# Relative bias added by VectorE, turned queries and probabilities, and prompt logits from raw rows

## The chip, the cores and the metric

The kernel runs on one core of one Trainium2 chip. The metric is the device time of one execution in microseconds (us). TensorE, VectorE, ScalarE and GpSimd compute, SyncE's queue issues the loads of the weights, and 16 DMA engines move them.

## The reference

One step of a two-layer trunk over 128 context tokens (the prompt, t = 0 in the kernel) and 128 latent tokens (the sample, t = 1), width 1024, all in float32. Layer 0 has grouped-query and differential attention, layer 1 neighbourhood attention of 16 heads: the sample's queries see 128 cached context keys and 128 latent keys inside a window, and the latent scores get a learned relative bias per head. Each layer ends in a mixture of 16 experts, two of them per token.

```python
s_lat = jnp.einsum('brqhd,brkhd->brhqk', qg, kw) * scale + bias   # then -inf outside the window
s_ctx = jnp.einsum('brqhd,bkhd->brhqk', qg, ctx_k) * scale
p = jax.nn.softmax(jnp.concatenate([s_ctx, s_lat], axis=-1), axis=-1)

h = rmsnorm(x, g) * (1.0 + scale_c) + shift_c      # per channel, from the condition
scores = jax.nn.softmax(h @ w_router, axis=-1)     # then the choice of group and of two experts
hid = silu(h @ w_gate[e]) * (h @ w_up[e]); y += gate * (hid @ w_down[e])
```

## The kernel before

Every engine has its own program, and semaphores join them. The weights, 486 MB in all, stream through a ring of six slots of 2 MB and a few borrowed buffers. SyncE's queue loads a slot as soon as the unit that held it has been read: `load` for dense units, `load_early` and `load_in_turn` for the experts' (L475), which wait for TensorE's count of finished units, `moe_used`. Experts come in eight pairs a layer: gather of the tokens (L932), gate and up products (L971), transposes, down products, scatter (L941).

Attention goes by eight turns a layer, four of the sample and then four of the prompt, four heads each. In turn j TensorE transposes the probabilities of j (`probs_transposed`, through `transposes`, L699), computes the scores of j + 2 (`scores`, L812 and L817), and multiplies the values of j (`values`, L855 or L863). VectorE takes the maxima (L1484), ScalarE the exponentials (L1211), VectorE the division by the sums (L1504), ScalarE the copies out of PSUM (L1222). Between these TensorE does the jobs that the table `FILL` writes down by hand: input projections, products of the modulation (`mod`, L721), output projections (`wo`, L770). The relative bias comes from memory with the queries of each grid row in reversed order. In layer 1's sample turns a product with the permutation `rev8` (which also holds 1/SCALE) turns each head's bias and adds it onto the scores in PSUM (L817).

Behind the last turn is the tail. For the sample: normed rows transposed (`hT`), modulated on the way out of PSUM, logits (`rt`, L875), transposes back into token rows (`hk`, L699). For the prompt, once the output projection has completed x: sum of squares on ScalarE (L1133), power on GpSimd, normed rows on VectorE (L1395), transposes on TensorE, modulation half on ScalarE (L1144) and half on VectorE (L1402), logits, maximum (L1411, L1412), exponential (L1152), and VectorE's choice of experts (L1594 to L1605). Then `positions` counts places in the expert lists (L888 to L892); in layer 1 it first issues 12 products that nobody reads (`keep_busy`, L743), and `experts` issues 8 more of them in front of the first gather. In layer 0 the products of the next layer's modulation stand among the tail's jobs, and its transposes (`nextT`, L732) ahead of `positions`. PSUM has one bank for sums, and seven are handed out in the order of the jobs; `EMPTIED_BY` names the engine that frees each.

## Time and profile before

| | us |
|---|---|
| median of 3 runs | 1283.19 |
| lowest and highest | 1282.77, 1284.61 |
| the profiled execution, its time | 1283.81 |
| its span on the core | 1282.0 |
| PE busy | 1183.7 (92%) |
| DVE busy | 279.4 (22%) |
| ACT busy | 188.4 (15%) |
| DMA, mean over the span | 383 GB/s |
| chain that ended last | PE 72%, DMA 18%, issue 5%, DVE 2% |

PE is TensorE, PEld its weight loads, DVE VectorE, ACT ScalarE, POOL GpSimd, SPq SyncE's queue. L with a number is a line of the kernel. A busy TensorE also holds the time in which a product is slower than it could be. The DMA share is the mean over the 16 engines; it reads 1.0 or a little over where they are full. PEclk is the granted clock of TensorE, 1.00 at 2.4 GHz and 0.50 at 1.2. A product of float32 operands is kept as two records, a transpose as one. Times of the trace are counted from the start of the span.

### The profile page before, as it was taken

How to read it: one execution, taken by the hardware profiler on the slowest of the kernel's cores; microseconds unless marked ns; L12 is line 12 of the kernel's file. 1: busy time of each engine (PE TensorE's matmuls, PEld its weight loads, DVE VectorE, ACT ScalarE, POOL GpSimd, SP SyncE). 2: the span in 40 equal slices, each digit the busy share in tenths (PEclk: the TensorE clock that was granted, in tenths of full speed). 3: DMA queues.
4: the chain of work that ended last, by engine and by line, in shares of the span. 5: the costliest groups of instructions: out<-in, count | busy, mean ns of one | idle time of the engine just before them, and what ended most of it. 6: DMA issues, size and time to landing. Idle time of an engine off the chain costs nothing.

```text
span 1282.0 us, 13868 instructions
## 1 busy us (share of the span) xinstructions
PE 1183.7 (92%) x5519; PEld 517.6 (40%) x5519; DVE 279.4 (22%) x672; ACT 188.4 (15%) x437; POOL 49.4 (4%) x57
## 2 busy tenths in 40 slices
PE   4999989999889898989899999999998899889898
PEld 2545454343333334333344554743433334343333
DVE  1156441201021010101413433412020110101013
ACT  1234221000000100000121342210000001000010
POOL 0502000000000000000011100000000000000000
PEclk9999999999999999999989999899999999999999
DMA  9959999999999999999991579889999999999995
GB/s 376 333 201 386 423 408 424 429 392 427 430 428 427 430 427 430 428 427 429 408 330 57 207 279 415 324 353 424 374 429 427 429 427 429 429 427 430 427 428 230
DMA packets 57647, 491.62 MB, mean 383 GB/s; under 512 B 5090, under 2 KB 6258, under 8 KB 26884
## 3 DMA queue, kind: packets, MB, share of 16 engines
q1 hardware_dynamic: 55408, 485.92, 91.4%
q0 software_dynamic: 2016, 4.94, 1.3%
q8 instruction: 29, 0.48, 0.1%
q10 hardware_dynamic: 180, 0.17, 0.0%
q14 instruction: 14, 0.11, 0.0%
HBM read 488.26 MB, written 2.75 MB: 383 GB/s over the span
## 4 chain that ended last, share of the span: by engine, by line
PE 72%; DMA 18%; issue 5%; DVE 2%; ACT 1%; SPq 1%; POOL 1%; DVEq 0%; ACTq 0%; POOLq 0%
PE bank L971 42%; DMA ring<-in_w_gate 11%; PE bank L752 11%; DMA ring<-in_w_up 5%; PE bank L770 3%; PE bank L941 3%; PE bank L932 3%; DMA ring<-in_w_in_ab 2%; PE bank L721 2%; PE bank L699 2%; PE bank L992 1%; PE bank L1021 1%; PE bank L812 1%; PE bank L1005 1%; PE bank L875 1%
## 5 line engine op out<-in xcount | busy, mean ns | idle before, releaser
L971 PE MATMUL bank<-ring,hT 128*64 128x512 f32 x2816 | 638.6, 608 | 63.7 <-issue 30.0
L971 PEld LDWEIGHTS bank<-ring,hT 128*64 128x64 f32 x2816 | 213.3, 140 | 464.5 <-issue 462.7
L752 PE MATMUL bank<-ring,hT 128*128 128x512 f32 (+1 forms) x352 | 149.5, 583 | 4.7 <-DMA ring<-in_w_in_ab 2.4
L752 PEld LDWEIGHTS bank<-ring,hT 128*128 128x128 f32 x352 | 67.1, 193 | 80.0 <-issue 76.6
L1694 DVE TENSOR_TENSOR work<-work,bank 128x512 f32<-128x512 f32 x56 | 38.5, 687 | 193.6 <-PE bank L941 193.4
L1687 DVE TENSOR_TENSOR work<-work,bank 128x512 f32<-128x512 f32 x32 | 22.0, 687 | 236.5 <-PE bank L971 236.5
L1728 DVE COPY work<-bank 128x512 f32<-128x512 f32 x16 | 11.1, 692 | 225.6 <-PE bank L971 209.3
L932 PE MATMUL bank<-work 128*128 128x128 f32 x512 | 59.8, 275 | 0.0
L932 PEld LDWEIGHTS bank<-work 128*128 128x128 f32 x512 | 58.6, 192 | 0.0
L770 PE MATMUL bank<-ring,work 128*128 128x512 f32 x128 | 56.3, 594 | 0.0
L1274 ACT ACTIVATE hT<-bank 128x512 f32<-128x512 f32 x32 | 19.0, 595 | 248.3 <-PE bank L1021 248.3
L941 PE MATMUL bank<-work 128*128 128x512 f32 x112 | 51.8, 605 | 0.0
L721 PE MATMUL bank<-ring,cond 128*32 128x512 f32 x384 | 47.0, 623 | 1.6 <-DMA ring<-in_w_mod 1.2
L1300 ACT ACTIVATE work<-bank 128x512 f32<-128x512 f32 x16 | 9.6, 597 | 220.3 <-PE bank L971 193.0
L1675 DVE TENSOR_TENSOR work<-work,bank 128x512 f32<-128x512 f32 x32 | 22.0, 688 | 83.4 <-ACT work L1283 83.4
L971 PE MATMUL bank<-work,hT 128*64 128x512 f32 x152 | 39.2, 593 | 0.0
L770 PEld LDWEIGHTS bank<-ring,work 128*128 128x128 f32 x128 | 23.8, 190 | 28.7 <-issue 28.6
L1287 ACT ACTIVATE work<-bank 128x256 f32<-128x256 f32 x16 | 6.2, 385 | 196.4 <-PE bank L1040 196.4
L1283 ACT ACTIVATE work<-bank 128x512 f32<-128x512 f32 x32 | 19.1, 597 | 94.5 <-PE bank L971 94.5
L941 PEld LDWEIGHTS bank<-work 128*128 128x128 f32 x112 | 20.1, 189 | 31.5 <-issue 31.5
L1211 ACT ACTIVATE work<-bank,nm 128x256 f32<-128x256 f32 (+1 forms) x64 | 26.1, 421 | 29.9 <-DVE nm L1486 29.9
L1420 DVE TENSOR_REDUCE hss<-bank 128x8 f32<-128x512 f32 (+1 forms) x16 | 10.5, 657 | 88.8 <-ACT bank L1170 88.8
(195 smaller groups left out, 688.5 us busy)
## 6 DMA issues: line engine op xcount, KB each, us to landing
ring<-in_w_gate SPq DMA_DIRECT2D x64, 2048.0 KB, 17.0
ring<-in_w_up SPq DMA_DIRECT2D x56, 2048.0 KB, 17.2
ring<-in_w_down SPq DMA_DIRECT2D x56, 2048.0 KB, 16.9
ring<-in_w_mod SPq DMA_DIRECT2D x23, 2048.0 KB, 11.9
work<-in_w_up SPq DMA_DIRECT2D x8, 2048.0 KB, 17.8
ring<-in_w_in_c SPq DMA_DIRECT2D x6, 2048.0 KB, 20.2
ring<-in_w_in_ab SPq DMA_DIRECT2D x4, 2048.0 KB, 21.5
ring<-in_w_down SPq DMA_DIRECT2D x8, 1024.0 KB, 16.3
```

Source lines behind the costliest of these rows:

```text
L699: ins = pe.transpose(b[:, i * P:(i + 1) * P], src, K("ident"))
L721: ins = pe.matmul(out, cond[:, 2 * k + r, :], cols, start=(k, r) == (0, 0), stop=(k, r) == (3, 1), tile_position=(0, 32 * j))
L752: ins = pe.matmul(b[:, 0:n], hT[:, c, t * P:(t + 1) * P], w[:, c, 0:n], start=c == 0, stop=c == DC - 1)
L770: ins = pe.matmul(b[:, :], oT(l, t, c), w[:, c, :], start=c == 0, stop=c == DC - 1)
L932: ins = pe.matmul(bank[h][:, c * P:(c + 1) * P], htok(t)[:, at:at + P], pick[:, t, :], start=t == 0, stop=t == 1)
L941: pe.matmul(bank[4 + 2 * t + h][:, :], GT[:, t, :], yd[:, h * UC:(h + 1) * UC], start=True, stop=True).then_inc(m["scattered"], 1)
L971: ins = pe.matmul(bank[banks[j]][64 * e:64 * e + 64, :], lhs[:, 4 * h + c, 64 * e:64 * e + 64], weights(e, c, j), start=(h, c) == (0, 0), ...
L1211: ins = act.activation(PR[:, j % 2, h, 0:nk], bank_of(("S", l, t, b, e))[:, i * nk:(i + 1) * nk], ACT.Exp, bias=nm[:, j % 2, h:h + 1], sca ...
L1283: act.activation(sg[:, h * UC:(h + 1) * UC], bank[h][:, :], ACT.Sigmoid).then_inc(m["sig_done"], 1)
L1675: dve.tensor_tensor(hid[:, half], sg[:, half], bank[h][:, :], ALU.mult).then_inc(m["gate_taken"], 1)
L1687: dve.tensor_tensor(hid[:, half], hid[:, half], bank[2 + h][:, :], ALU.mult).then_inc(m["hid_done"], 1)
L1694: dve.tensor_tensor(y[:, t, cols], y[:, t, cols], bank[4 + 2 * t + h][:, :], ALU.add).then_inc(m["y_added"], 1)
```

## The change

The bias is masked and scaled once on VectorE with keys as they lie and queries still reversed, so the queries are reversed instead: in layer 1's sample the transposes of the queries (two banks, eight chunks) become products with the permutation `rev`, and so rows of scores come out reversed. VectorE adds the bias to the scores in PSUM before it takes the maxima, and the products with the bias go. The transposes of these turns' probabilities become products with `rev` too, which puts the order right.

In both layers the prompt's logits no longer wait for its normed and modulated rows. Raw rows of x are transposed (`xT`) and copied by ScalarE and VectorE, a bank each; the router's weights are scaled once by the modulation's scale (`wr0`), and the products of its shift with the router's weights (`rc`) are added after the logits have been multiplied by the rows' inverse norm. The modulation of the prompt's rows (`hT`, all eight parts now on ScalarE) and its token rows (`hk`) come behind the logits. In layer 1 the sample's logits move ahead of the second half of the prompt's output projection. In layer 0 `nextT` moves behind `positions`, and VectorE's part of it behind the count of rounds. `keep_busy` is as it was.

The core of the diff, without the context lines and the new declarations:

```diff
-    block("rev8")[:] = (row == back[None, :]) / SCALE
+    block("rev")[:] = row == back[None, :]
...
-    block("negrev")[:] = np.where(inside, 0.0, MASKED * SCALE)[back, :]
+    block("negrev")[:] = np.where(inside, 0.0, MASKED)[back, :]
...
-        7: [("hT", 1, 1), ("wo", 0, 0), ("rt", 1), ("wo", 1, 0), ("mod", 1, 0, 1),
-            ("hT", 1, 0), ("mod", 1, 0, 2), ("rt", 0), ("mod", 1, 0, 3), ("nextT",), ("pos",)]},
+        7: [("hT", 1, 1), ("wo", 0, 0), ("rt", 1), ("wo", 1, 0), ("rc",), ("mod", 1, 0, 1), ("xT",), ("mod", 1, 0, 2),
+            ("rt", 0), ("hT", 1, 0), ("mod", 1, 0, 3), ("hk", 0), ("pos",), ("nextT",)]},
...
-        7: [("hT", 1, 1), ("wo", 0, 0), ("wo", 1, 0), ("rt", 1), ("hT", 1, 0), ("rt", 0), ("pos",)]}}
+        7: [("hT", 1, 1), ("wo", 0, 0), ("rt", 1), ("wo", 1, 0), ("rc",), ("xT",),
+            ("rt", 0), ("hT", 1, 0), ("hk", 0), ("pos",)]}}
...
     def engine(name):
...
-            return ("act", "dve")[name[4]]
+            return "act" if name[2:4] == (1, 0) else ("act", "dve")[name[4]]
+        if kind == "xT":
+            return ("act", "dve")[name[2]]
+        if kind == "rt":
+            return ("dve", "act")[name[2]]
...
+            def turned(name, parts):
...
+                b = bank_free(name)
+                for i, src in enumerate(parts):
+                    ins = pe.matmul(b[:, i * P:(i + 1) * P], src, K("rev"), start=True, stop=True)
+                ins.then_inc(filled, 1)
...
+                if (l, t) == (1, 1):
+                    pe.wait_ge(ld_const, 16)
...
-                    transposes(("T", l, t, i), p)
+                    (turned if (l, t) == (1, 1) and i < 2 else transposes)(("T", l, t, i), p)
...
-                biased = (l, t) == (1, 1)
-                if biased and j == 0:
-                    pe.wait_ge(ld_const, 16)
-                    pe.wait_ge(bias_masked, 1)
...
-                                        start=True, stop=not biased, tile_position=(64 * e, 0))
-                        if i == 1 and not biased:
-                            ins.then_inc(filled, 1)
-                    for e in range(2) if biased else ():
-                        ins = pe.matmul(banks[e][:, i * nk + P:(i + 1) * nk], K("rev8"), bias[:, 4 * b + 2 * i + e, :],
-                                        start=False, stop=True)
+                                        start=True, stop=True, tile_position=(64 * e, 0))
...
-                    transposes(("PT", l, t, b, k), [PR[:, j % 2, h, kc * P:(kc + 1) * P] for kc, h in chunks[k * per:(k + 1) * per]])
+                    (turned if (l, t) == (1, 1) else transposes)(
+                        ("PT", l, t, b, k), [PR[:, j % 2, h, kc * P:(kc + 1) * P] for kc, h in chunks[k * per:(k + 1) * per]])
...
             def logits(l, t):
...
+                if t == 0:
+                    pe.wait_ge(router_scaled, l + 1)
...
-                    pe.wait_ge(*emptied_by(("hT", l, 1, t, h)))
+                    pe.wait_ge(*emptied_by(("hT", l, 1, 1, h) if t else ("xT", l, h)))
...
-                    ins = pe.matmul(b[:, 0:NE], hT[:, c, t * P:(t + 1) * P], wr[:, c, :], start=c == 0, stop=c == DC - 1)
+                    ins = pe.matmul(b[:, 0:NE], hT[:, c, t * P:(t + 1) * P], (wr if t else wr0)[:, c, :], start=c == 0, stop=c == DC - 1)
...
+                if t == 1:
+                    token_rows(l, 1)
...
+            def token_rows(l, t):
...
+                    pe.wait_ge(*emptied_by(("hT", l, 1, t, h)))
...
+            def shift_logits(l):
...
+                pe.wait_ge(mod_ready, 2 * l + 2)
+                pe.wait_ge(ld_router, 32)
+                b = bank_free(("rc", l))
+                for c in range(DC):
+                    ins = pe.matmul(b[:, 0:NE], modc[:, l, 2, 0, c:c + 1].to_broadcast([P, P]), wr[:, c, :], start=c == 0, stop=c == DC - 1)
+                ins.then_inc(filled, 1)
...
+            def rows_transposed(l):
+                pe.wait_ge(x_ready, 8 * l + 4)
+                for h in range(2):
+                    transposes(("xT", l, h), [channels(x[:, 0, :], 4 * h + i) for i in range(4)])
...
-                last = number["pos", l]
+                last = number["modT", 1, 0] if l == 0 else number["pos", 1]
...
-                for c in range(4):
-                    ins = act.activation(hT[:, c, t * P:(t + 1) * P], bank_of(name)[:, c * P:(c + 1) * P], ACT.Identity,
+                for c in range(8 if (kind, t) == (1, 0) else 4):
+                    if c == 4:
+                        ins.then_inc(emptied["act"], 1)
+                        name = ("hT", l, 1, 0, 1)
+                        act.wait_ge(filled, fill(name))
+                    ins = act.activation(hT[:, c, t * P:(t + 1) * P], bank_of(name)[:, c % 4 * P:(c % 4 + 1) * P], ACT.Identity,
...
+            def rows_transposed(l):
+                name = ("xT", l, 0)
+                act.wait_ge(filled, fill(name))
+                act.activation(hT[:, 0:4, 0:P], bank_of(name)[:, :].rearrange("p (c q) -> p c q", c=4), ACT.Copy).then_inc(emptied["act"], 1)
...
             def router(l, t):
...
-                name = ("rt", l, t)
...
-                act.activation(sco[:, t, :], bank_of(name)[:, 0:NE], ACT.Exp, bias=st2[:, t:t + 1],
-                               accum_out=st2[:, 2 + t:3 + t]).then_inc(emptied["act"], 1)
-
+                ins = act.activation(sco[:, t, :], bank_of(("rt", l, 1))[:, 0:NE] if t else lg[:, :], ACT.Exp, bias=st2[:, t:t + 1],
+                                     accum_out=st2[:, 2 + t:3 + t])
+                ins.then_inc(emptied["act"] if t else prompt_scored, 1)
...
+            def token_rows(l, t):
...
-                if l == 0:
-                    router(0, 1)
+                router(l, 1)
+                token_rows(l, 1)
...
-                if l == 1:
-                    router(1, 1)
+                rows_transposed(l)
+                router(l, 0)
...
-                router(l, 0)
...
+                token_rows(l, 0)
...
+                if group == 2:
+                    dve.wait_ge(mod_ready, 2 * l + 2)
+                    dve.wait_ge(ld_router, 32)
+                    dve.tensor_tensor(wr0, wr[:, :, :], modc[:, l, 3, 0, :].unsqueeze(2).to_broadcast([P, DC, NE]), ALU.mult).then_inc(router_scaled, 1)
...
+            def prompt_rows(l):
...
+                name = ("rc", l)
+                dve.wait_ge(filled, fill(name))
+                dve.tensor_copy(rc[:, :], bank_of(name)[:, 0:NE]).then_inc(emptied["dve"], 1)
+                name = ("xT", l, 1)
+                dve.wait_ge(filled, fill(name))
+                dve.tensor_copy(hT[:, 4:8, 0:P], bank_of(name)[:, :].rearrange("p (c q) -> p c q", c=4)).then_inc(emptied["dve"], 1)
...
             def largest_logit(l, t):
...
-                then(dve.tensor_reduce(st2[:, t:t + 1], bank_of(name)[:, 0:NE], AX.X, ALU.max))
+                if t == 0:
+                    dve.wait_ge(*emptied_by(("rc", l)))
+                    dve.scalar_tensor_tensor(out=lg[:, :], in0=bank_of(name)[:, 0:NE], scalar=ss[:, 0:1], in1=rc[:, :],
+                                             op0=ALU.mult, op1=ALU.add).then_inc(emptied["dve"], 1)
+                    dve.wait_ge(*emptied_by(name))
+                then(dve.tensor_reduce(st2[:, t:t + 1], bank_of(name)[:, 0:NE] if t else lg[:, :], AX.X, ALU.max))
...
-                dve.tensor_tensor(bias, bias, K("negrev").unsqueeze(1).to_broadcast([P, 16, P]), ALU.add).then_inc(bias_masked, 1)
+                dve.scalar_tensor_tensor(out=bias, in0=bias, scalar=1.0 / SCALE, in1=K("negrev").unsqueeze(1).to_broadcast([P, 16, P]),
+                                         op0=ALU.mult, op1=ALU.add).then_inc(bias_masked, 1)
...
+                if (l, t) == (1, 1):
+                    if j == 0:
+                        dve.wait_ge(bias_masked, 1)
+                    for e in range(2):
+                        name = ("S", l, t, b, e)
+                        dve.wait_ge(filled, fill(name))
+                        s = bank_of(name)[:, 0:2 * nk].rearrange("p (h k) -> p h k", h=2)[:, :, P:2 * P]
+                        ins = dve.tensor_tensor(s, s, bias[:, 4 * b + e:4 * b + e + 3:2, :], ALU.add)
+                    then(ins)
...
             def router(l):
...
-                for t in range(TT):
-                    dve.wait_ge(*emptied_by(("rt", l, t)))
+                dve.wait_ge(*emptied_by(("rt", l, 1)))
+                dve.wait_ge(prompt_scored, l + 1)
...
-                if l == 0:
-                    mod(1, 0)
...
+                if l == 0:
+                    mod(1, 0)
...
-                if l == 0:
-                    largest_logit(0, 1)
+                largest_logit(l, 1)
...
-                if l == 1:
-                    largest_logit(1, 1)
+                prompt_rows(l)
...
-                modulate(l, 1, 0)
...

```

## Rows read from the trace of the kernel before

**Rows 1.** Windows, layer 1: busy us (instructions) per engine, PEclk, DMA share, GB/s

```profile
675.00:700.00 25.00, 25.00 (x78) 12.52 (x77) 9.02 (x8) 4.95 (x10) 5.46 (x1) 1.00 0.00 1
...
828.00:837.00 9.00, 9.00 (x52) 4.17 (x50) 0.00 (x0) 1.19 (x2) 0.00 (x0) 1.00 0.17 66
...
900.00:930.00 30.00, 30.00 (x160) 12.99 (x158) 2.06 (x3) 2.88 (x5) 0.00 (x0) 1.00 0.91 370
```

**Rows 2.** Windows of layer 0's first pairs, same columns

```profile
200.00:260.00 60.00, 60.00 (x290) 23.22 (x288) 10.88 (x20) 5.65 (x10) 0.00 (x0) 1.00 1.01 429
...
260.00:290.00 30.00, 30.00 (x160) 12.86 (x158) 2.06 (x3) 2.88 (x5) 0.00 (x0) 1.00 0.95 387
```

**Rows 3.** Timeline of SyncE's queue: start us, us, instruction

```profile
814.44 0.39 SPq L523 DMA_DIRECT2D m<-in_w_down  x1
...
837.19 0.80 SPq L475 DMA_DIRECT2D ring<-in_w_down  x2
```

**Rows 4.** Timeline, TensorE in attention: start, us, instruction, idle before it

```profile
85.72 2.00 PE L812 MATMUL bank<-work 64*128 64x256 f32 x16
...
724.74 1.04 PE L699 MATMUL bank<-const,work 128*128 128x128 f32 x8
...
725.71 0.70 PE L812 MATMUL bank<-work 64*128 64x256 f32 x4
...
728.25 1.09 PE L863 MATMUL bank<-work 128*64 128x128 f32 x16
...
749.46 1.04 PE L699 MATMUL bank<-const,work 128*128 128x128 f32 x8
```

**Rows 5.** Timeline of VectorE in layer 1's attention, same columns

```profile
728.28 1.27 DVE L1484 TENSOR_REDUCE nm<-bank 128x2 f32<-128x512 f32 x2
...
741.12 0.42 DVE L1513 COPY work<-bank 128x256 f32<-128x256 f32 x1
```

**Rows 6.** Timeline of layer 1's tail, all engines, same columns

```profile
808.17 1.85 PE L875 MATMUL bank<-wr,hT 128*128 128x16 f32 x16
...
809.16 0.69 DVE L1538 TENSOR_TENSOR x<-x,tmp 128x512 f32<-128x512 f32 x1
...
809.87 1.07 PE L699 MATMUL bank<-const,hT 128*128 128x128 f32 x8
...
812.35 1.15 PE L699 MATMUL bank<-const,tmp 128*128 128x128 f32 x8 [1.42 <-DVE tmp L1395]
...
813.16 1.51 ACT L1144 ACTIVATE hT<-bank,modc 128x128 f32<-128x128 f32 x4 [1.32 <-PE bank L699]
...
815.08 3.57 PE L875 MATMUL bank<-wr,hT 128*128 128x16 f32 x16 [1.58 <-ACT hT L1144]
...
818.89 0.15 DVE L1412 TENSOR_SCALAR st<-st 128x1 f32<-128x1 f32 x1
...
820.22 3.29 PE L743 MATMUL bank<-const 128*128 128x128 f32 x24
...
823.41 0.40 PE L888 MATMUL bank<-chosen,const 128*128 128x16 f32 x2
...
826.41 3.74 PE L932 MATMUL bank<-work 128*128 128x128 f32 x32
```

**Rows 7.** Windows around the clock's fall and rise, columns of rows 1

```profile
814.00:815.00 1.00, 0.00 (x0) 0.00 (x0) 0.98 (x4) 0.67 (x2) 0.00 (x0) 0.67 0.73 307
...
821.00:822.00 1.00, 1.00 (x10) 1.00 (x9) 0.90 (x5) 0.07 (x1) 0.00 (x0) 0.92 1.06 442
```

**Rows 8.** Timeline of layer 0's tail, TensorE

```profile
169.80 1.92 PE L721 MATMUL bank<-ring,cond 128*32 128x512 f32 x16
...
173.89 1.15 PE L699 MATMUL bank<-const,tmp 128*128 128x128 f32 x8 [2.17 <-DVE tmp L1395]
...
183.59 0.37 PE L888 MATMUL bank<-chosen,const 128*128 128x16 f32 x2 [0.57 <-issue]
...
186.57 3.74 PE L932 MATMUL bank<-work 128*128 128x128 f32 x32
```

More of the change, by code:

```diff
@@ L43 @@
 for _name, _n in (("ident", P), ("mhalf", HD),
-                  ("upper", P), ("ones", P), ("iota", CAP), ("selg", 8), ("rev8", P),
+                  ("upper", P), ("ones", P), ("iota", CAP), ("selg", 8), ("rev", P),
                   ("negrev", P), ("low4", 16), ("cos", HD), ("ssin", HD), ("thr", ROUNDS_MAX - 1),
@@ L150, in banks_of @@
         return [("hT", l) + rest + (h,) for h in range(2)]
+    if kind == "xT":
+        return [("xT", l, h) for h in range(2)]
+    if kind == "hk":
+        return [("hk", l, rest[0], h) for h in range(2)]
     if kind == "rt":
-        return [("rt", l, rest[0])] + [("hk", l, rest[0], h) for h in range(2)]
+        return [("rt", l, rest[0])] + (banks_of(l, ("hk", 1)) if rest[0] else [])
     return [(kind, l) + rest]
@@ L164 @@
 EMPTIED_BY = {"vecT": "dve", "bT": "dve", "modT": "dve", "T": "act", "S": "act", "PT": "act",
-              "O": "dve", "oT": "act", "gb": "act", "wo": "dve", "hk": "act", "rt": "act", "pos": "dve"}
+              "O": "dve", "oT": "act", "gb": "act", "wo": "dve", "hk": "act", "rc": "dve", "pos": "dve"}
 def pt_jobs(l, t, b):
@@ L206, in engine @@
         if kind == "hT":
-            return ("act", "dve")[name[4]]
+            return "act" if name[2:4] == (1, 0) else ("act", "dve")[name[4]]
+        if kind == "xT":
+            return ("act", "dve")[name[2]]
+        if kind == "rt":
+            return ("dve", "act")[name[2]]
         if kind == "qkv":
@@ L247, in build @@
         br = sb("br", [P, NE])
+        rc = sb("rc", [P, NE])
+        lg = sb("lg", [P, NE])
         ss = sb("ss", [P, 4])
@@ L264, in build @@
         cnt8 = sb("cnt8", [P, TT * NG])
+        wr0 = cmq[:, :].rearrange("p (c e) -> p c e", c=DC)
         rounds = sb("rounds", [P, 1], I32)
@@ L353, in build @@
         max_ready, shared, o_ready = (sem(n) for n in ("max_ready", "probs_shared", "o_ready"))
+        prompt_scored = sem("prompt_scored")
+        router_scaled = sem("router_scaled")
         logit_max, mask_ready, rounds_ready = (sem(n) for n in ("logit_max", "mask_ready", "rounds_ready"))
@@ L894, in meanwhile @@
             def meanwhile(l, point):
-                job = {"in": project, "modT": mod_transposed, "gb": gate_rows, "wo": out_project, "rt": logits,
+                job = {"in": project, "modT": mod_transposed, "gb": gate_rows, "wo": out_project, "rt": logits, "hk": token_rows,
                        "oT": outputs_transposed, "hT": norm, "T": heads_transposed, "pos": positions}
@@ L901, in meanwhile @@
                         mod_transposed(1, 0)
+                    elif item[0] in ("rc", "xT"):
+                        {"rc": shift_logits, "xT": rows_transposed}[item[0]](l)
                     else:
```

## Prediction

> **What bounds the kernel now.** I read four views in this order. The windows by stage show first where the DMA engines stand still. In layer 1 they are idle for the whole of 675 to 700 and for most of 828 to 837, and 9% short between 900 and 930, while TensorE's share is full in all three [rows 1]. In layer 0 they are at 1.01 up to 260 and only from 260 to 290 a little short, 0.95 of 30 us, some 1.5 us [rows 2]. Where the DMA is full the weights set the pace, and an earlier TensorE is worth nothing there; time comes off only where the DMA waits for TensorE. The queue of SyncE, second, says what ends the large hole: after the load of 814.44 the next one goes out at 837.19, when the first product of pair 0 has given its slot back [rows 3]. So a shift of layer 1's first product by X moves that load, and with it all that follows, by X, in either direction; a gain is passed on up to about 8 us. In layer 0 a later first product is passed on too, since the DMA is already caught at 260 to 290, an earlier one by 1.5 us at most. Third, TensorE's rows of layer 1's attention have no gap but the few tenths of us before L863, so there its own work counts [rows 4, 5]. Fourth, the tail from the output projection to the gather: waits on VectorE and ScalarE, and a stretch at half clock [rows 6, 7].
>
> **Layer 1's attention.** Removed: 16 products with the bias. A turn of scores with them runs from 725.71 to the values' products at 728.25, 2.5 us [rows 4]; layer 0's two turns without them take 2.00, 1.0 a turn [rows 4]. Four turns: 4 x 1.5 = 6.0 us less. Added: 40 chunks (8 of queries, 32 of probabilities) are turned by a full product in place of a transpose. Eight transposes take 725.71 - 724.74 = 0.97 us, 0.12 each [rows 4]. The nearest product of that shape is the gather, 32 records for 16 products in 3.74 us, 0.23 each [rows 6]; the trace keeps two records for a float32 product and one for a transpose. So 40 x 0.11 = 4.4 us more. The lower end is nothing (if a turn costs what a transpose does), the upper the pace of the bias products, 0.3 each, +7.5 us; I take the gather's row, since it too runs one 128x128 product after another. Net -1.6 us.
>
> The Trainium skill, "TensorE: Matmul & The Clock Gate" (Terms), says that transpose mode is four times faster for float32. By that rule a turned chunk costs four transposes, 0.48 us, and the edit adds 40 x 0.36 = 14.4 us. The gather's row stands against it with not quite twice, and the row decides; the rule stays as a rival.
>
> VectorE gets two additions a turn over 128x256 of a score bank, 0.42 each by the copy of that size out of PSUM [rows 5], and a wait behind them: some 0.95 us a turn between scores and maxima. Queued behind it are the maxima (0.64 us each), the exponentials and, a turn later, the transposes. I cost it at nothing: scores of turn 2 are read at 728.28 and their transposes start only at 749.46, behind two projections of 7 us [rows 4, 5]; turns 0 and 1 have such projections in front too, turn 3 (scores at 737, transposes 754) one of them. Without that cover it would be 4 x 0.95 = 3.8 us. The mask becomes one operation in place of one: nothing. The scaled router weights wr0 (one more operation on VectorE in layer 1's scale group) stand just ahead of the last copy that the output projection waits for: about 0.35 us later, from 0.2 to 0.4. In layer 0 it is under cover. Attention: -1.6 + 0.35 = -1.25 us.
>
> **Layer 1's tail, in the times of before.** The logits of the sample and their token rows, 809.87 - 808.17 = 1.70 and 0.97 us, move ahead of the second half of the output projection; x is complete 2.67 us later, at 809.85 + 2.67 = 812.5 [rows 6]. The shift's logits (16 records, 1.70) fill TensorE up to then: nothing. Eight transposes of x to 813.5; ScalarE and VectorE copy a bank each (0.7), VectorE to 814.45; logits of the prompt on TensorE 814.45 to 816.15, at full clock. Before, they began at 815.08 and took 3.57 at half clock [rows 6]. Maximum, exponential, selection: before, the sign change is at 818.89, 0.4 after the logits, and the first product of the positions at 823.41, 4.52 later [rows 6]. After, with one operation more, the sign change is at 816.8 and the choice is ready at 821.3, 2.1 us earlier. But positions now stands behind something else. VectorE's copy and three small operations put the normed rows at 816.2, their transposes end at 817.15, the exponential leaves ScalarE at 817.3, and ScalarE alone now does the eight modulations, 3.0 us where it did four in 1.51 beside VectorE's four [rows 6]: to 820.35. The second four transposes of token rows end at 820.95. Then come the 12 idle products ahead of the positions (L743, 24 records), which the diff leaves, 12 x 0.23 = 2.8 us: to 823.75. Positions start at 823.75 against 823.41, and from there to the gather it is 3.0 us as before. Tail: +0.35 us. The gain of the raw rows is lost behind the modulations and the idle products.
>
> **Layer 0.** The output projection ends at 169.80 [rows 8]; shift logits to 171.5, modulation products (1.9) to 173.4, transposes of x to 174.35, modulation products to 176.25, logits to 177.95, sign change 178.6, choice 183.15. Transposes, the third modulation products, ScalarE's eight modulations (to 182.2) and the last token rows end at 182.8, so the positions go at 183.2 against 183.59. The transposes of the next layer's modulation, before in front of the positions, now lie behind them: 183.2 + 1.1 + 0.5 + 1.9 for the eight idle products = 186.7 against 186.57 for the gather [rows 8]. +0.1 us.
>
> **Moved waits.** SyncE's last load but one waits for the transposes of the prompt's normed rows, about 4 us later than before against the tail's own times; behind it is the m4 load, and the queue then waits for 837 anyway [rows 3]. The hole of the DMA begins only at about 828 [rows 1], so this costs nothing; without that cover, up to 2 us. VectorE's modT of the next layer moves behind the slots, beside the first product: nothing.
>
> **Sum.** -1.25 + 0.35 + 0.1 = -0.8 us. The profiled execution has a span of 1282.0 and a time of 1283.81, 0.6 above the median of 1283.19; the same shift from the median gives 1282.4.
>
> **The rivals.**
> 1. Half clock ahead of the positions. Before, TensorE's clock falls to 1.2 GHz after 814 and is back at 2.4 after 821, following gaps before 812.35 and 815.08 with only eight transposes between [rows 6, 7]. After, the gaps are at 813.5 (1.0 us) and then, longer, 1.8 and 1.0 us between 817.15 and 820.45 while ScalarE modulates. If the clock falls there, the idle products and the positions run at half speed. The spell of before cost 1.7 (logits) + 0.9 (token rows) + 0.4 (idle products) = 3.0 us. Then 1282.4 + 3.0 = 1285.4, up to 1286.5 where the whole of it falls on idle products and positions. It decides as soon as the pause from the transposes to the token rows is enough to drop it. For it: two such pauses dropped it. Against it: layer 0 has a pause of 2.17 us in its tail [rows 8], and its products behind it run at their full pace.
> 2. The choice sets the positions. If ScalarE's modulations are done sooner than I think, the tail gives up to -2.1 in place of +0.35: 1282.4 - 2.45 = 1279.9. Against it, the program's order.
> 3. Turning costs four transposes (the page's rule, as above): +10.0 on my sum, 1292.4.
> 4. VectorE's additions are not covered in attention: up to +3.8, 1286.2.
>
> **How the numbers follow.** Forecast 0.52 at 1282.4, its own range 1281 to 1284; clock rival 0.30, half of it beyond the bound; choice 0.08 and other gains 0.03; four transposes 0.03; VectorE 0.04. A difference under 0.2% (2.6 us: 1280.6 to 1285.8) can't be told from none. Faster 0.12, same 0.67, slower 0.21. The range 1279.8 to 1286.6 takes in the clock and the choice, and leaves out the rule.
>
> **What would show it.** Right: scores of layer 1's first turns at 1.0 us, turned chunks at 0.23; logits of the prompt at full clock; the choice of layer 1 ready some 2 us before TensorE reaches the positions, the idle products between. Layer 0's gather within 0.5 us of 186.57. Layer 1's gather about 0.8 us earlier than 826.41 and the load after pair 0's first product as much. Wrong: L743 at half clock in front of the positions; turned chunks over 0.3; gaps in front of the turned probabilities with VectorE as releaser; or a last product that does not move with the gather.

## The result and the profile after

| | before | after |
|---|---|---|
| median | 1282.82 | 1284.86 |
| lowest and highest of 20 runs each | 1279.03, 1284.61 | 1281.94, 1289.15 |
| after to before, 95% interval | | 1.0021 (1.0012 to 1.0031) |
| the profiled execution, its time | 1283.81 | 1281.97 |
| its span | 1282.0 | 1280.2 |

The change makes the kernel slower by 2.7 us by the ratio (1.5 to 4.0), 2.0 by the medians. I had forecast 1282.4, 0.8 us less than before. The range, 1279.8 to 1286.6, held the time, but the sign was wrong. Of the values that I had written down, the first rival's 1285.4 lies nearest.

The profiled execution of after is 1.8 us *shorter* than that of before, against the sign of the medians. Split at three starts that every trace has:

| stretch | before | after | difference |
|---|---|---|---|
| start to layer 1's first input projection | 644.35 | 643.13 | -1.22 |
| from there to the first product of the prompt's output projection | 150.01 | 148.75 | -1.26 |
| from there to layer 1's first gather | 32.05 | 33.81 | +1.76 |
| from there to the end | 455.6 | 454.5 | -1.1 |

The first and last stretch differ by as much between two profiles of one kernel (the last is 455.6 and 454.1 in two profiles of before, 454.5 and 454.5 in two of after). So neither profile's total says what the change did. The two middle stretches hold the changed work of layer 1, but they too can hold more or less time at half clock, so I compare them over all profiles below.

The page of after, busy time of the engines and the chain that ended last:

```profile
PE 1186.5 (93%) x5575; PEld 521.8 (41%) x5575; DVE 282.5 (22%) x680; ACT 192.6 (15%) x447; POOL 49.4 (4%) x57
...
PE 74%; DMA 19%; issue 3%; DVE 2%; ACT 1%; SPq 1%; POOL 0%; DVEq 0%; ACTq 0%
```

TensorE has 2.8 us more than before and the chain leans on it a little more; nothing here names a place. The timeline of TensorE in layer 1's attention, after (start, us, instruction, idle before it), and under it VectorE's:

```profile
704.74 2.00 PE L831 MATMUL bank<-work 64*128 64x256 f32 x16
...
720.51 1.95 PE L720 MATMUL bank<-const,work 128*128 128x128 f32 x16
722.38 1.13 PE L831 MATMUL bank<-work 64*128 64x256 f32 x8
...
738.00 7.10 PE L773 MATMUL bank<-ring,hT 128*128 128x512 f32 x16 [0.62 <-issue]
...
791.88 7.10 PE L791 MATMUL bank<-ring,work 128*128 128x512 f32 x16 [0.28 <-DVE work L1589]
...
706.70 0.75 DVE L1554 TENSOR_TENSOR bank<-bank,gbuf 128x256 f32<-128x256 f32 x2
```

Against [rows 4]: two turns of scores in 2.00 us, as layer 0's; eight turned chunks (L720, 16 records) from 720.51 to 722.38, 1.87 us or 0.23 each. No gap stands before them. VectorE's two additions take 0.75 us, and for turn 0 TensorE is at a projection until 720.51. Behind turn 3 there is a new gap of 0.62 ahead of a projection, which comes back in every profile with the new attention and in none with the old. The output projection waits 0.28 for the copy behind the scaled router weights.

The projection behind the gap takes the PSUM bank that turn 3's first pair of score heads has to leave: it is the seventh bank handed out after it. In after ScalarE is done with that bank at 737.90, and TensorE starts at 738.00. In before the same projection followed TensorE's transposes without a gap (the first line is of after, the second of before):

```profile
737.70 0.20 ACT L1259 ACTIVATION_READ_ACCUMULATOR work<-bank,nm 128x1 f32 x1
...
742.59 7.03 PE L752 MATMUL bank<-ring,hT 128*128 128x512 f32 x16
```

From the end of turn 3's scores to ScalarE's first exponential it is 1.48 us in before (739.76 to 741.24) and 2.49 in after (734.39 to 736.88). So VectorE's additions, 1.0 us with the wait behind them, are not covered here: from the transposes (740.79 and 735.41) to the projection it is 1.80 us before and 2.59 after.

The first input projection of layer 1 differs too, and no edit touches it. Before, then after:

```profile
644.35 10.16 PE L752 MATMUL bank<-ring,hT 128*128 128x512 f32 x16 [2.26 <-DVE hT L1402]
...
643.13 9.19 PE L773 MATMUL bank<-ring,hT 128*128 128x512 f32 x16 [2.07 <-DVE hT L1454]
```

It starts at half clock in both; the clock is back at 2.4 GHz 6.2 us behind its start in before and 4.2 in after. From its start to the transposes behind it there are 9.99 and 9.03 us. A second profile of before has 9.13, and one of a kernel with the new attention (layer 0 undone, layer 1 filled, below) has 9.89. So 0.96 of the 1.26 in the table above is no effect of the change. From those transposes to the output projection it is 140.02 in both profiles of before and 139.71 or 139.72 in all eight with the new attention and layer 1's new tail: 0.30 us less.

Layer 1's tail after, TensorE with the lines of other engines that set it, against [rows 6]:

```profile
812.14 1.93 PE L892 MATMUL bank<-cmq,hT 128*128 128x16 f32 x16 [0.94 <-ACT hT L1193]
813.92 1.43 PE L713 MATMUL bank<-const,tmp 128*128 128x128 f32 x8
815.08 2.88 ACT L1186 ACTIVATE hT<-bank,modc 128x128 f32<-128x128 f32 x8
816.61 1.12 PE L713 MATMUL bank<-const,hT 128*128 128x128 f32 x4 [1.26 <-ACT hT L1186]
818.01 1.11 PE L713 MATMUL bank<-const,hT 128*128 128x128 f32 x4 [0.28 <-ACT hT L1186]
818.92 4.03 PE L764 MATMUL bank<-const 128*128 128x128 f32 x24
818.96 0.19 DVE L1681 SCALAR_TENSOR_TENSOR chosen<-cnt,top 128x32 f32<-128x32 f32 x1
822.79 0.29 PE L924 MATMUL bank<-chosen,const 128*128 128x16 f32 x2
...
825.69 3.74 PE L970 MATMUL bank<-work 128*128 128x128 f32 x32
836.47 0.80 SPq L489 DMA_DIRECT2D ring<-in_w_down  x2
```

and the windows around it, columns as in [rows 7] (PEclk, DMA share and GB/s are the last three):

```profile
813.00:815.00 2.00, 2.00 (x18) 1.95 (x17) 1.17 (x4) 0.23 (x2) 0.00 (x0) 0.90 0.93 397
815.00:817.00 2.00, 0.73 (x4) 0.39 (x3) 1.56 (x7) 2.00 (x8) 0.00 (x0) 0.50 0.97 366
817.00:819.00 2.00, 1.72 (x9) 1.32 (x8) 1.72 (x11) 1.44 (x4) 0.00 (x0) 0.50 1.13 462
819.00:821.00 2.00, 2.00 (x11) 2.00 (x11) 1.18 (x9) 0.60 (x1) 0.00 (x0) 0.50 1.05 451
821.00:823.00 2.00, 2.00 (x19) 2.00 (x17) 0.00 (x0) 0.00 (x0) 0.00 (x0) 0.90 0.98 418
828.00:837.00 9.00, 9.00 (x49) 3.86 (x50) 0.07 (x1) 1.02 (x3) 0.00 (x0) 1.00 0.18 69
```

The choice of experts starts at 818.96. The positions (L924), which need it, start 3.83 us later, at 822.79, behind the token rows (L713, 1.12 and 1.11 for four transposes that take 0.66 at full clock) and the 12 idle products (L764, 4.03). From 815 to 821 the clock is at 1.2 GHz. This is the sign that I had written down for the first rival. The load that had waited for pair 0's first product goes out at 836.47, against 837.19 [rows 3]: 0.72 for a gather that is 0.72 earlier. So the step "a shift of the first product moves the load by as much" holds.

### The profile page after: what moved, and what is told of

It is laid out like the page before. It is cut to its first block, busy times and chain, and to the rows that moved or that the text cites. A ratio compares the mean times of both kernels' runs of the same rounds, so it can differ in the third digit from the quotient of the medians.

```text
span 1280.2 us, 14016 instructions
## 1 busy us (share of the span) xinstructions
PE 1186.5 (93%) x5575; PEld 521.8 (41%) x5575; DVE 282.5 (22%) x680; ACT 192.6 (15%) x447; POOL 49.4 (4%) x57
## 4 chain that ended last, share of the span: by engine, by line
PE 74%; DMA 19%; issue 3%; DVE 2%; ACT 1%; SPq 1%; POOL 0%; DVEq 0%; ACTq 0%
PE bank L1009 42%; PE bank L773 11%; DMA ring<-in_w_gate 10%; DMA ring<-in_w_up 7%; PE bank L791 4%; PE bank L979 3%; PE bank L970 3%; DMA ring<-in_w_in_ab 2%; PE bank L742 2%; PE bank L713 1%; PE bank L1030 1%; PE bank L1059 1%; PE bank L831 1%; PE bank L720 1%; PE bank L1043 1%
## 5 line engine op out<-in xcount | busy, mean ns | idle before, releaser
L1259 ACT ACTIVATE work<-bank,nm 128x256 f32<-128x256 f32 (+1 forms) x64 | 26.0, 420 | 30.6 <-DVE nm L1562 30.6
```

The lines of the kernel that those rows point to most:

```text
L1259: ins = act.activation(PR[:, j % 2, h, 0:nk], bank_of(("S", l, t, b, e))[:, i * nk:(i + 1) * nk], ACT.Exp, bias=nm[:, j % 2, h:h + 1], sca ...
```

## The experiments

The idle products and their number are no part of what is computed, and no kernel below leaves out a part of the computation. Each ratio is against before, run in turn on the same chip. Beside the times stand two readings of each profile, counted from the first product of the prompt's output projection: the choice of experts (VectorE) and the first gather, layer 1.

| kernel | median us | ratio (95%) | choice | gather | layer 1's tail |
|---|---|---|---|---|---|
| before | 1282.82 | | 28.80 | 32.05 | old |
| before again | 1281.47 | 0.9999 (0.9987 to 1.0011) | 27.18 | 30.63 | old |
| attention alone | 1282.49 | 1.0004 (0.9994 to 1.0015) | 28.80 | 33.32 | old |
| layer 1's tail undone | 1282.98 | 1.0003 (0.9987 to 1.0018) | 27.24 | 30.64 | old |
| after | 1284.86 | 1.0021 (1.0012 to 1.0031) | 27.08 | 33.81 | new |
| after again | 1284.35 | 1.0017 (1.0006 to 1.0029) | 27.07 | 33.78 | new |
| tails alone | 1285.03 | 1.0028 (1.0015 to 1.0040) | 27.16 | 33.53 | new |
| layer 0's tail undone | 1285.00 | 1.0029 (1.0019 to 1.0040) | 27.07 | 33.81 | new |
| pauses filled | 1283.90 | 1.0005 (0.9992 to 1.0019) | 26.96 | 32.10 | new |
| 12 idle products out | 1282.85 | 1.0008 (0.9997 to 1.0019) | 27.08 | 33.17 | new |
| pauses filled, 12 out | 1280.61 | 0.9987 (0.9974 to 1.0000) | 26.96 | 31.35 | new |
| layer 0 undone, layer 1 filled | 1281.99 | 1.0001 (0.9989 to 1.0013) | 26.96 | 30.21 | new |
| both tails filled | 1280.37 | 0.9989 (0.9978 to 0.9999) | 26.97 | 30.22 | new |
| attention alone, old tails filled | 1280.42 | 0.9991 (0.9980 to 1.0002) | 27.17 | 31.26 | old |

### The two kernels again, and the two halves of the change

No edit: the changed kernel and, in the next set, the one before.

> The changed kernel once more, to see its spread and, if it comes, a profile of one of its longer executions. Theory A (half clock in layer 1's tail, longer in some executions): median 1284 to 1286 with a spread of 5 us or more, the kernel before 1281 to 1284; a long execution shows more time at half clock between the prompt's logits and the first gather, up to 7 us of it. Theory B (the added work is simply longer than I summed): every execution of the changed kernel some 2 us longer, with a spread like the kernel before.

> The kernel before as it is, for a second profile of it and its spread. If my sum went by an execution whose tail of layer 1 was at its slow end (3.0 us of half clock in it), other executions of it have less of that, and the median is near 1282.4 with single executions at 1279 to 1281. If the half clock is always there, the profile shows the same 32.05 us from the output projection to the gather.

The change of attention with both tails as before, and the reverse. Of the attention edit the core is

```diff
-                    transposes(("T", l, t, i), p)
+                    (turned if (l, t) == (1, 1) and i < 2 else transposes)(("T", l, t, i), p)
...
-        7: [("hT", 1, 1), ("wo", 0, 0), ("rt", 1), ("wo", 1, 0), ("rc",), ("xT",),
-            ("rt", 0), ("hT", 1, 0), ("hk", 0), ("pos",)]}}
+        7: [("hT", 1, 1), ("wo", 0, 0), ("wo", 1, 0), ("rt", 1), ("hT", 1, 0), ("rt", 0), ("pos",)]}}
```

(the first hunk against before, the second against after) and the tails alone have neither `turned` nor the additions:

```diff
-                    (turned if (l, t) == (1, 1) else transposes)(
+                    transposes(
...
-                        ins = dve.tensor_tensor(s, s, bias[:, 4 * b + e:4 * b + e + 3:2, :], ALU.add)
```

> Only the attention part: bias on VectorE, queries and probabilities turned; the tails of both layers as before. Theory A: the attention gives 1.6 us less, and the clock pattern of the tail is that of before, so 0 to 2 us faster than before. A rival (turned products or VectorE's additions cost more than summed): 1 us or more slower than before.

> Only the tails of both layers: raw rows for the prompt's logits and the new order; attention as before. Theory A: it holds the whole loss, 2 to 4 us slower than before, with a wide spread. The rival that the loss is in the attention: within 1 us of before.

The loss is repeated (1.0017) and sits in the tails: alone they cost 3.6 us by the ratio (1.9 to 5.1), while attention alone is within the measurement of nothing (-0.8 to +1.9). In its trace the attention stretch is 1.67 us shorter than before's (148.34 against 150.01), but 1.05 of that lies in the first input projection (8.94 against 9.99). Behind that projection it is 139.40 against 140.02: attention brings 0.62 us, not the 1.6 of my sum. The scores are 6.0 us shorter and the 40 turned chunks 4.6 longer, near my 6.0 and 4.4; the gap behind turn 3, with the tenths around it, takes back 0.8. The scaled router weights cost 0.32 (140.34 with the tails alone against 140.02, and 139.72 against 139.40). A gain of 0.62 is too small for these times to show. The tail of this profile, TensorE:

```profile
812.14 3.56 PE L876 MATMUL bank<-wr,hT 128*128 128x16 f32 x16 [1.58 <-ACT hT L1145]
815.54 1.95 PE L699 MATMUL bank<-const,hT 128*128 128x128 f32 x8
817.28 4.71 PE L750 MATMUL bank<-const 128*128 128x128 f32 x24
821.84 0.29 PE L889 MATMUL bank<-chosen,const 128*128 128x16 f32 x2
```

Here the clock is at half from 811 to 821 in an unchanged tail, and the tail is 33.32. The second profile of before shows the same instructions otherwise:

```profile
812.87 1.94 PE L875 MATMUL bank<-wr,hT 128*128 128x16 f32 x16 [1.58 <-ACT hT L1144]
814.64 1.95 PE L699 MATMUL bank<-const,hT 128*128 128x128 f32 x8
816.39 3.65 PE L743 MATMUL bank<-const 128*128 128x128 f32 x24
819.87 0.29 PE L888 MATMUL bank<-chosen,const 128*128 128x16 f32 x2
...
822.77 3.74 PE L932 MATMUL bank<-work 128*128 128x128 f32 x32
...
819.32 0.19 DVE L1605 SCALAR_TENSOR_TENSOR chosen<-cnt,top 128x32 f32<-128x32 f32 x1
```

The logits take 1.94, not the 3.57 of [rows 6]; the clock falls only behind them, under the token rows and the idle products. That half clock costs nearly nothing, since VectorE's choice is ready at 819.5 and the idle products end as it does. Old tails lie at 30.63, 30.64, 32.05 and 33.32, by where the clock falls; new ones at 33.5 to 33.8, all four. Means 31.66 and 33.73: +2.1 us, on four profiles a side, of which the old ones spread over 2.7. And the choice, counted alike, comes at 27.0 to 27.2 in every new tail and at 27.2 in an old one whose logits run at full clock. My trace of before held an old tail in its middle, and I took its half-clock logits for the old tail's own length.

### Which tail

```diff
-        7: [("hT", 1, 1), ("wo", 0, 0), ("rt", 1), ("wo", 1, 0), ("rc",), ("xT",),
-            ("rt", 0), ("hT", 1, 0), ("hk", 0), ("pos",)]}}
+        7: [("hT", 1, 1), ("wo", 0, 0), ("wo", 1, 0), ("rt", 1), ("hT", 1, 0), ("rt", 0), ("hk", 0), ("pos",)]}}
```

for layer 1 undone, and the like in layer 0:

```diff
-        7: [("hT", 1, 1), ("wo", 0, 0), ("rt", 1), ("wo", 1, 0), ("rc",), ("mod", 1, 0, 1), ("xT",), ("mod", 1, 0, 2),
-            ("rt", 0), ("hT", 1, 0), ("mod", 1, 0, 3), ("hk", 0), ("pos",), ("nextT",)]},
+        7: [("hT", 1, 1), ("wo", 0, 0), ("rt", 1), ("wo", 1, 0), ("mod", 1, 0, 1),
+            ("hT", 1, 0), ("mod", 1, 0, 2), ("rt", 0), ("hk", 0), ("mod", 1, 0, 3), ("nextT",), ("pos",)]},
```

> The changed kernel with layer 1's tail put back to the order and the operations of before; layer 0's tail and the attention part as changed. Theory C (layer 1's tail holds the loss): the median falls to 1281 to 1282.5. Theory D (layer 0's tail holds it, by a clock that falls more often ahead of its first gather and is passed on): it stays at 1284 to 1285.

> The changed kernel with layer 0's tail put back; layer 1's tail and the attention part as changed. In the profiles so far layer 0's new tail takes 17.15 us from the output projection to the gather, or 18.7 where the clock falls ahead of it, against 16.8. If the three parts simply add up (layer 0 some 1.1 us, layer 1's tail some 2, attention -1.4), the mean is about 1 us under the changed kernel's 1285, at 1283.5 to 1284.5. The rival that all of the loss is in layer 1's tail: no change from 1285.

With layer 1's tail undone the ratio is 1.0003, with layer 0's undone 1.0029, as without. The two intervals just miss each other (up to 1.0018, from 1.0019), though they come from different sets. This points to layer 1's tail; the pair of kernels that settles it, taken in one set, stands in the last group below. In layer 0 the traces show a small one too: the gather of after starts 17.16 us after the output projection's end (169.75), 16.77 in [rows 8]. TensorE, after:

```profile
182.23 0.66 PE L713 MATMUL bank<-const,hT 128*128 128x128 f32 x4 [0.54 <-ACT hT L1186]
183.47 0.37 PE L924 MATMUL bank<-chosen,const 128*128 128x16 f32 x2 [0.58 <-issue]
...
184.58 0.71 PE L753 MATMUL bank<-const,m 128*128 128x128 f32 x4
185.12 1.95 PE L764 MATMUL bank<-const 128*128 128x128 f32 x16
186.91 3.74 PE L970 MATMUL bank<-work 128*128 128x128 f32 x32
```

The modulation's transposes and the eight idle products, 2.3 us together, are the last thing before the gather; the second bank of token rows and the positions each wait 0.5 ahead of them, the one for ScalarE. In three of the seven profiles with this tail (tails alone, layer 1's tail undone, and pauses filled with 12 out) those last products ran at half clock, and the tail took 18.7 us. Tails alone:

```profile
186.38 1.09 PE L746 MATMUL bank<-const,m 128*128 128x128 f32 x4
187.26 3.05 PE L757 MATMUL bank<-const 128*128 128x128 f32 x16
190.15 3.07 PE L969 MATMUL bank<-work 128*128 128x128 f32 x26
```

One of six old tails of layer 0 had such a stretch (18.4, attention alone with old tails filled): there the clock fell right behind the pause of 2.17 us, and the transposes and the modulation products behind it took 1.83 and 2.87 in place of 1.15 and 1.92.

### The clock, and the idle products

Filled: 3 idle products ahead of the prompt's logits and 5 and 1 ahead of the two banks of token rows, where TensorE waits for ScalarE. The 12 are kept or taken out.

```diff
+                if (l, t) == (1, 0):
+                    pe.wait_ge(mod_emptied, 6)
+                    keep_busy(3)
...
+                    if (l, t) == (1, 0):
+                        keep_busy((5, 1)[h])
```

```diff
-                    keep_busy(12)
```

> The changed kernel with idle products in TensorE's pauses of layer 1's tail (3 ahead of the prompt's logits, 5 and 1 ahead of the two banks of its token rows), none of which is longer than its pause by more than 0.2 us; the 12 ahead of the positions stay. Theory A: the clock holds, the 12 run in 2.8 us in place of up to 5.2, and the time is 2 to 4 us under the changed kernel with a narrower spread. Theory B: no gain, or 0.5 us slower.

> The changed kernel without the 12 idle products ahead of layer 1's positions. If they are what stands between the choice (ready at 819.15 in the profile of the changed kernel) and the positions (822.79), the positions go at 819.2 to 820, and the time is 2.5 to 3.5 us lower, if the clock is up again by the first gather; if the clock then stays at half into pair 0, the gain is under 1.5 us.

> Pauses filled as in the run with filled pauses, and the 12 idle products left out. If clock and idle products add up: 2.8 us under that run, 1280.5 to 1281.5, and faster than the kernel before. If only one of them matters: within 1 us of it.

TensorE with the pauses filled and the 12 kept, and a window of it:

```profile
816.88 1.28 PE L764 MATMUL bank<-const 128*128 128x128 f32 x10
...
820.51 2.84 PE L764 MATMUL bank<-const 128*128 128x128 f32 x24
823.19 0.29 PE L929 MATMUL bank<-chosen,const 128*128 128x16 f32 x2
...
817.00:819.00 2.00, 1.55 (x14) 1.36 (x13) 1.56 (x7) 2.00 (x8) 0.00 (x0) 1.00 0.94 348
```

The clock stays at 2.4 GHz, the 12 take 2.84 in place of 4.03, and the tail is 32.10 in place of 33.81: half clock costs the new tail 1.7 us. The times are less clear: 1.5 us less than after again by the ratios, 0.5 by the medians, where I had expected 2 to 4, and the spread is no narrower (6.5 us). The choice has not moved (26.96), and the positions still start 2.24 behind it. With the 12 out and no filling TensorE reads:

```profile
820.88 0.58 PE L923 MATMUL bank<-chosen,const 128*128 128x16 f32 x2 [0.27 <-DVE chosen L1680]
...
823.01 3.67 PE L764 MATMUL bank<-const 128*128 128x128 f32 x16
```

Now the choice sets the positions, 3.4 us sooner into the tail than in after (27.53 against 30.91). But the clock isn't back, and positions (0.43 apart in place of 0.22) and the eight idle products before the gather (3.67 in place of 2.03) run at half speed, so 2.7 of the 3.4 is given back: 33.17. The two have to be done together. In times: filling alone 1.0005 and the 12 out alone 1.0008, neither clearly below the changed kernel's 1.0017 to 1.0021; both together 0.9987, its interval wholly below that of after, though in its one trace the clock still fell behind the positions (31.35).

### Both tails filled, and the 12 cut to 2

Layer 1 filled 3, 5 and 1, with 2 idle products in place of the 12; in one kernel layer 0's tail is the old one, in the other it is the new one with 2 idle products ahead of its second bank of token rows and 2 ahead of the positions, into banks that these jobs own; a third has attention alone and old tails, with 6 idle products ahead of layer 1's transposes of normed rows and 7 ahead of its logits.

```diff
+                    if (l, t, h) == (0, 0, 1):
+                        pe.wait_ge(*emptied_by(jobs[number["hk", 0, 0, 1] - 7][0]))
+                        keep_busy(2, bank_of(("hk", 0, 0, 1)))
...
-                    keep_busy(12)
+                    keep_busy(2)
+                else:
+                    pe.wait_ge(*emptied_by(jobs[number["pos", 0] - 7][0]))
+                    keep_busy(2, bank_of(("pos", 0)))
```

> As the run before, and in layer 1's tail the pauses filled with idle products (3, 5, 1) and 2 in place of the 12 ahead of the positions. If it is the clock and the idle products that cost: from the output projection to the gather 30 us in place of 33.8, and 1279.5 to 1281, faster than the kernel before by 1.5 to 3 us. If the order itself costs: not under 1282.

> The changed kernel with both tails filled: layer 1 as in the run before, layer 0 with 2 idle products ahead of the second bank of token rows and 2 ahead of the positions. If those 4 keep the clock up in layer 0, its tail takes 17.2 us in every execution and the mean is 1280 to 1281.5; if not, it is 1 us above the run before.

> The attention part alone with the tails of before, and layer 1's two pauses filled with 6 and 7 idle products. If the clock is the price of the pauses in the old tail too, it is held through the logits, the tail takes 30.6 us and the mean is 1280 to 1281; then nothing of the new tail is needed for a gain. If the fill only adds work: 1282.5 to 1283.5.

Both tails filled, TensorE, then VectorE's choice and SyncE's load, and the window of the DMA's hole:

```profile
819.97 0.61 PE L764 MATMUL bank<-const 128*128 128x128 f32 x4
820.66 0.39 PE L935 MATMUL bank<-chosen,const 128*128 128x16 f32 x2
...
823.67 3.74 PE L981 MATMUL bank<-work 128*128 128x128 f32 x32
...
820.42 0.19 DVE L1692 SCALAR_TENSOR_TENSOR chosen<-cnt,top 128x32 f32<-128x32 f32 x1
...
834.44 0.81 SPq L489 DMA_DIRECT2D ring<-in_w_down  x2
...
828.00:837.00 9.00, 9.00 (x44) 2.92 (x42) 1.63 (x8) 1.70 (x3) 0.00 (x0) 1.00 0.52 177
```

The positions start 0.24 behind the choice, the tail is 30.22, 3.6 us shorter than after's, the load goes out at 834.44, and the DMA's share from 828 to 837 is 0.52, in after 0.18. Counted by microseconds, it is under a tenth busy for 3 us (832 to 835), against 8 in before (830 to 838) and 6 in its second profile (828 to 834). The ratio to before is 0.9989 (0.9978 to 0.9999), 1.4 us less than before and 4.1 less than after by the ratios, and its 12 runs lie closest together (1278.23 to 1282.32). Its median is the lowest, but only just clear of before, picked out of several, and not to be told from the one with the pauses filled and the 12 out (0.9987).

The kernel with layer 0's tail undone and layer 1's filled missed its forecast of 1279.5 to 1281: it came to 1281.99 and a ratio of 1.0001, though its tail is as short (30.21). It can't be told from the one with both filled (0.9989 to 1.0013 against 0.9978 to 0.9999), so what layer 0's order adds to it is open. Against the kernel that differs from it by the fill alone, layer 0's tail undone, it does settle the question above: both ran in one set on one chip, the tail goes from 33.81 to 30.21, and the ratio from 1.0029 (from 1.0019) to 1.0001 (up to 1.0013), in the means of the runs 3.5 us (1284.85 and 1281.33). Layer 1's tail is 3.6 us shorter in the trace, and within the noise the time is shorter by as much.

Attention alone with old tails filled comes to 0.9991 (0.9980 to 1.0002), near the fastest, so a gain would not need the new tails. Its pauses held the clock through the logits (1.93), but its tail took 31.26, not the 30.6 that I had expected: the positions wait 1.16 for the choice, and behind them the clock fell (eight idle products in 2.92).

## Why the prediction was wrong, step by step

- **Attention: the prices right, the cover wrong.** Scores without the bias products 1.0 a turn, a turned chunk 0.23, the scaled router weights 0.32 against 0.35: these terms came as summed. The stretch of 1.26 in the first pair of profiles looks like the 1.25 forecast, but that is luck, since 0.96 of it is the longer time at half clock in before's first input projection. Behind that projection attention brings 0.30 (0.62 without the scaled router weights), forecast 1.25 and 1.6. The step that failed is "I cost it at nothing" for VectorE's additions. I had looked for cover in front of the turned probabilities, and there it held; but turn 3's scores also hold a PSUM bank that a projection takes, and it came 0.8 us later. So rival 4 came true in part, 0.8 of its 3.8.
- **Rival 3 fell.** The rule of the Trainium skill, "TensorE: Matmul & The Clock Gate" (Terms), that transpose mode is four times faster for float32, would make it 0.48 a chunk, an estimate from four of the trace's 0.12; the trace has 0.23 against 0.12, not quite twice.
- **The DMA's hole: right.** The load follows pair 0's first product one to one, 0.72 for 0.72 in after.
- **The choice of layer 1: the number right, the comparison wrong.** I had it 2.1 us earlier than in the trace of before. It is 1.7 earlier (27.08 against 28.80), but only against that trace, whose logits ran at half clock. Against a tail whose logits didn't (27.18), the raw rows bring 0.1: the logits start at 20.26 in place of 20.73, and the longer way to the choice takes 0.37 of that back.
- **The step that failed most: the tail's length, "+0.35".** It set a new tail at full clock against an old one that held a half-clock stretch, 33.81 and 32.05 in these two traces, +1.76. Against the other old tails it is +2.1 (means of four). Of the 1.4 that was missed in the first pair, the 12 idle products account for 1.1 (3.87 from their start to the positions, against my 2.8) and a start of them 0.45 us later than I had it for the rest (27.04 into the tail against 26.59; the second bank of token rows ahead of them takes 1.11 in place of 0.66); from the positions to the gather it is 0.1 less than I had. The prediction's own rows had both facts: the half clock in [rows 7], and that in the old tail the idle products (820.22) end where the choice is ready. I said that the gain was lost behind them but not that the new order puts them in the open, where each us that they grow is a us of the kernel. That is the mechanism of rival 1, which I gave 0.30 and a price of 3.0 against a measured 1.7 (33.81 against 32.10 filled); the other 1.5 of the loss against an old tail whose logits ran at full clock (32.10 against 30.63) has no half clock in the new tail: the positions stand 2.24 behind the choice.
- **What spoke against rival 1 was no good evidence.** I set it low since layer 0 has a pause of 2.17 us in its tail at full pace behind it [rows 8]. There products of the modulation, 1.9 us each, stand between the small ones, and layer 1's tail has none; that this is why it held is not shown. And layer 0 falls too, in three of seven new tails, and once right behind that same pause of 2.17 in an old one.
- **Layer 0: +0.39 where +0.1 was forecast**, and 1.6 more at times. Taking it back did not lower the time, so this part is below what the runs can tell.
- **The sum.** -0.3 + 2.1 + 0.4 is +2.2, and with some 0.4 for layer 0's stretches (1.6 in 3 of 7, against 1 of 6, too few to be sure of) +2.6; by the ratio it is +2.7 (1.5 to 4.0). Nothing of size is left over, though the 2.1 rests on four profiles a side.

What stays open: why the clock falls in one execution and not in another at the same pauses (old tails 30.6, 32.1 and 33.3); whether layer 0's stretches at half clock come more often in its new tail; and whether attention alone is worth its 0.62 us in the times, which the ratio of 1.0004 (0.9994 to 1.0015) can neither show nor exclude.

## What to carry to other kernels

Count a stage in several traces of the same kernel before a fraction of a per cent is forecast from it: one profile may hold more half clock than the next, and a gain measured from it is then too large. Here it spoiled the forecast of the tail and made the first reading of attention look right. Attention cut where no such spell can reach, from the transposes behind the first input projection, repeats to 0.03 us. When work is moved ahead of a step, look at who arrives last at the next joint afterwards, and at who waits for each buffer that the moved work holds, not only for its result. In this tail, idle products that end as VectorE's choice is ready cost nothing, the same ones in an order where the choice is already there cost all of their length, at the slower clock. Here they paid in the pauses, where they held the clock, and not behind them.

## What the hardware showed that I had not expected

- In layer 1's tail, where only transposes and products of 16 columns stand between pauses of 0.3 to 1.6 us, the granted clock fell to 1.2 GHz in all eight unfilled profiles listed above that keep the 12 idle products. Nine idle products in the pauses (some 2 us of work) held it at 2.4 up to the positions in all four profiles that have them; in the one without the 12 it fell behind the positions. The page "TensorE: Matmul & The Clock Gate" of the Trainium skill (Part 1) says that the throttled state is the default and activity releases it; the filled and unfilled traces agree.
- Where in the tail it falls varies: old tails are 30.63 to 33.32 long with the same instructions. A like stretch, between 24 and 39 us, stands in nine of the fourteen profiles, of either order, and in these layer 0's output projection ends 1.3 to 4.4 us later than in after. Layer 1's first input projection starts at 642.9 to 644.4 us where neither this stretch nor one in layer 0's tail is there, at 643.9 to 645.3 with the first alone, and at 646.4 to 649.2 with both. That is as large as the spread of a kernel whose 20 runs cover 5.6 to 7.2 us; how much of that spread it makes is not measured.
